# Expert value sums of a two-block network: which operand stands still in TensorE

## What is computed

```
def _peer(x, wq, k1, k2, u_tab, v_tab):      # x: 256 tokens x 1024; u_tab, v_tab: 16384 experts x 1024
    eidx, gate = ...                          # 8 heads x 16 chosen experts a token, softmax gates
    ub = jnp.take(u_tab, ib, axis=0)
    act = gelu(einsum('td,tkd->tk', xb, ub))
    vb = jnp.take(v_tab, ib, axis=0)
    return einsum('tk,tkd->td', gb * act, vb)
h = _layer_norm(ALPHA * h + _peer(h, ...), ln2_g, ln2_b)
```

## Time and profile before

| | us |
|---|---|
| median of three timed runs | 2996.52 |
| lowest, highest | 2991.83, 2996.59 |
| span of the profiled execution, first to last instruction | 2991.0 |
| TensorE matmuls busy | 2928.9 (98%) |
| TensorE weight loads busy | 2599.6 (87%) |
| VectorE busy | 2125.5 (71%) |
| ScalarE busy | 1498.7 (50%) |
| POOL busy | 686.6 (23%) |

### The profile page before, as it was taken

The page is one execution under the profiler, slowest core; times in us unless marked ns, Lnnn a source line. Parts: engine busy times, 40 slices in busy tenths (PEclk is TensorE's granted clock), DMA queues, the critical chain, the costliest instruction groups (busy, mean ns, idle before and its releaser), DMA issues.

```text
span 2991.0 us, 54746 instructions
## 1 busy us (share of the span) xinstructions
PE 2928.9 (98%) x18452; PEld 2599.6 (87%) x18452; DVE 2125.5 (71%) x3656; ACT 1498.7 (50%) x2410; POOL 686.6 (23%) x443
## 2 busy tenths in 40 slices
PE   8999999999999999999999999999999999999998
PEld 7888888888878888899999978888899999978887
DVE  6667576766766667758986677777758986767776
ACT  4456444444655445445555545455545555544544
POOL 0002100000021002117778400000207777500000
PEclk9999999999999999999999999999999999999999
DMA  6545455555463554457887777776446888777775
GB/s 222 189 162 187 159 167 186 169 189 189 148 219 119 184 185 149 155 174 206 197 212 186 194 253 241 242 239 195 165 160 198 195 208 199 179 245 243 239 243 189
DMA packets 255982, 581.52 MB, mean 194 GB/s; under 512 B 61336, under 2 KB 127168, under 8 KB 255344
## 3 DMA queue, kind: packets, MB, share of 16 engines
q1 hardware_dynamic: 210656, 547.94, 56.6%
q0 software_dynamic: 45200, 31.93, 7.0%
HBM read 542.92 MB, written 36.84 MB: 194 GB/s over the span
## 4 chain that ended last, share of the span: by engine, by line
PE 81%; DVE 12%; ACT 3%; issue 2%; DMA 1%; POOL 1%; SPq 0%; ACTq 0%; DVEq 0%
PE acc L783 32%; PE work L719 23%; PE work L729 10%; PE work L731 5%; DVE wsp L456 4%; PE acc L847 3%; PE acc L1203 2%; ACT wsp L453 2%; PE acc L1340 1%; DMA ring<-in_stream 1%; DVE rows_sb L2474 1%; ACT scratch L1419 1%; DMA back<-second_dram 1%; PE work L1125 0%; POOL st L583 0%
## 5 line engine op out<-in xcount | busy, mean ns | idle before, releaser
L456 DVE TENSOR_TENSOR wsp<-ring,wsp 128x1024 fp32r<-128x1024 f32 x908 | 1105.3, 1225 | 562.2 <-ACT wsp L453 558.0
L453 ACT ACTIVATE wsp<-ring 128x1024 fp32r<-128x1024 f32 x944 | 984.9, 1052 | 498.6 <-PE work L719 238.3
L719 PE MATMUL work<-xsp,wsp 128*128 128x256 f32 x7872 | 971.7, 285 | 6.2 <-DVE wsp L456 3.2
L783 PE MATMUL acc<-wsp,hsp 128*128 128x512 f32 x4128 | 956.0, 390 | 9.9 <-DVE hsp L2674 8.0
L719 PEld LDWEIGHTS work<-xsp,wsp 128*128 128x128 f32 x7872 | 953.8, 192 | 11.3 <-DVE wsp L456 4.8
L783 PEld LDWEIGHTS acc<-wsp,hsp 128*128 128x128 f32 x4128 | 769.2, 188 | 173.7 <-issue 9.6
L729 PE MATMUL work<-xsp,wsp 128*128 128x512 f32 x1408 | 503.8, 400 | 6.7 <-DVE xsp L1859 5.5
L687 POOL DMA_INDIRECT second_dram<-rows_sb,spots x256 | 472.9, 1847 | 146.3 <-issue 88.7
L731 PE MATMUL work<-xsp,wsp 128*128 128x256 f32 x1408 | 395.7, 281 | 0.0
L583 POOL TENSOR_TENSOR st<-st,mhalf 128x1 f32<-128x1 f32 x24 | 20.6, 864 | 1561.7 <-DVE st L1879 805.1
L729 PEld LDWEIGHTS work<-xsp,wsp 128*128 128x128 f32 x1408 | 265.2, 188 | 75.0 <-DVE xsp L1859 6.6
(11 more groups left out here) (355 smaller groups left out, 2138.9 us busy)
## 6 DMA issues: line engine op xcount, KB each, us to landing
ring<-in_stream SPq DMA_DIRECT2D x944, 512.0 KB
back<-second_dram SPq DMA_DIRECT2D x256, 128.0 KB, 3.2
second_dram<-back POOLq DMA_DIRECT2D x32, 512.0 KB, 13.3
second_dram<-arena SPq DMA_DIRECT2D x184, 64.0 KB
rows_sb<-in_rows POOLq DMA_DIRECT2D x10, 512.0 KB, 6.8
second_dram<-acts SPq DMA_DIRECT2D x72, 64.0 KB
second_dram<-rows_sb,spots POOLq DMA_INDIRECT x256
h_saved_dram<-h POOLq DMA_DIRECT2D x2, 1024.0 KB, 5.0
```

Of the source, the lines that this page charges most:

```text
L453: self.eng.activation(dst[:, 0, :], src, ACT.Copy).then_inc(high_done, 1)
L456: self.eng.tensor_tensor(dst[:, 1, :], src, dst[:, 0, :].bitcast(F32), ALU.subtract)\
L719: mm = pe.matmul(out_, lhsT=w[:, a, 128 * c:128 * c + 128], rhs=xsp[:, b, c, :], start=(c == 0 and n == 0), stop=(c == DC - 1 and n == 2))
L783: mm = pe.matmul(ACC[2 * b + n][:, :], lhsT=act[:, pa, 128 * b:128 * b + 128], rhs=w[:, pw, 512 * n:512 * n + 512], start=(first and m == ...
```

## The change

The expert layers' value stage gets its own unit, in the wide form. For each of the eight 128-column pieces c of the width, the high piece of the value unit is stationary and the 512 columns of `hsp` (high and low parts of 256 tokens) move; then the low piece is stationary and the 256 high columns move. So there are 8 pairs, 16 matmuls and 16 weight loads a unit, and the result lies with the width on the partitions: eight sums of 128 x 512, one in each of the eight banks. The stage therefore claims the four `W` banks too, before its first unit.

At the end three steps are new. ScalarE copies columns 256 to 511 of each bank, the part of the low activations, to `arena` (`second_half`). VectorE adds them to columns 0 to 255 (`columns_sum`). TensorE turns the eight sums back with 16 transposes of 128 x 128 into the four `ACC` banks, where `add_block` finds them as before. The last wait of `add_block` is now given by its caller. The other callers pass the same wait as before.

```diff
+        class ValueSum(Group):
+            def bank(self, c):
+                return ACC[(0, 2, 1, 3)[c]] if c < 4 else W[(self.k + c) % 4]
+            def claim_all(self, pe):
+                for q in range(4):
+                    self.claim(pe, q)
...
                 pe.wait_ge(g_moved, GROUPS * (l + 1))
+                G.claim_all(pe)
 
                 def value_unit(i, first, last, it=None):
                     n = 0 if it is None else it
                     pe.wait_ge(act_low, n * 6 + (TILES + NKEYS * l + i + 1))
-                    down_unit(G, i, hsp[:, i % 2, :, :], first, last, 6 * n)
+                    w = G.unit(pe, i, 6 * n)
+                    a = hsp[:, i % 2, :, :]
+                    for c in range(DC):
+                        o = G.bank(c)
+                        pe.matmul(o[:, :], lhsT=w[:, 0, 128 * c:128 * c + 128], rhs=a.rearrange("p s t -> p (s t)"),
+                                  start=first, stop=False)
+                        mm = pe.matmul(o[:, 0:T], lhsT=w[:, 1, 128 * c:128 * c + 128], rhs=a[:, 0, :],
+                                       start=False, stop=last)
+                        if last and c < DC - 1:
+                            mm.then_inc(ev("value_column"), 1)
+                    mm.then_inc(unit_done, 1)
...
+                for c in range(DC):
+                    G.wait_added(pe, max(c, 1), l)
+                    if c == 4:
+                        G.wait_added(pe, 3, l)
+                    n, k = c // 4, c % 4
+                    for b in range(NB):
+                        mm = pe.transpose(ACC[2 * b + n][:, 128 * k:128 * k + 128],
+                                          columns_sum[:, c, 128 * b:128 * b + 128], ident)
+                        if c == 3:
+                            mm.then_inc(ev("half_block"), 1)
+                        elif c == DC - 1:
+                            mm.then_inc(ev("value_turned") if b else ev("first_block"), 1)
...
                 split.upto(G.u + 129)
+                G = ValueSum(part, "V")
+                for c in range(DC):
+                    if c < DC - 1:
+                        act.wait_ge(ev("value_column"), (DC - 1) * l + c + 1)
+                    else:
+                        G.ready_unit(act, NKEYS - 1)
+                    act.activation(second_half[:, c, :], G.bank(c)[:, T:2 * T], ACT.Copy).then_inc(ev("half_copied"), 1)
                 ln_squares()
...
                 dve.wait_ge(h_back, 16 * (l + 1))
+                V = ValueSum(part, "V")
+                for c in range(DC):
+                    dve.wait_ge(ev("half_copied"), DC * l + c + 1)
+                    V.added(tt(columns_sum[:, c, :], second_half[:, c, :], V.bank(c)[:, 0:T], ALU.add), c)
                 dve.memset(st[:, 31:32], 0.0).then_inc(side_free, 1)
-                layer_norm(3 * l + 3, part, (V, NKEYS - 1))
+                layer_norm(3 * l + 3, part, lambda eng: eng.wait_ge(ev("value_turned"), l + 1))
```

26 lines of the change are left out of this document (19 added, 7 removed).

## The result

The changed kernel took 3026.4 us, the median of 4 runs (3023.29 to 3032.19); in the same series the kernel before took 2995.89 us (2991.83 to 2996.59). The ratio is 1.0105, 95% interval 1.0093 to 1.0117: 1.05% slower. The forecast was 3026.8.

A forecast was written before the change was run, and what follows sets the result against it. TensorE's matmul issue was taken to bound the value stage. Units 25.0, start 0, clock -1.6 and ends 6.9 add 30.3 us to the 2991.0 span; with 5.5 around it, 3026.8 us, range 3013 to 3037.

The forecast's parts named there:

- The units: Value units: eight long-short pairs at 0.3525 us make 2.82 us a unit against 2.72, adding 25.0 us in both layers.
- Rival (a): Value units: the mixed stream runs in its quicker rhythm, 0.347 us a pair, giving 3017 us; chance 20%.
- (b): Value units: bank changes and waits at a unit's head add time, giving 3039 us, or 3033 at half; chance 12%.
- (c): Value units: extra matmuls cost nothing, 0.340 us a pair, giving 3001.8 us; 6% stated for this and (d).
- (d): Value stage: the change misses its aim, for example because transfers bound it, giving 3002 us; 6% stated with (c).
- The start: Value stage's start: claiming the work banks delays the first units 1.7 us, hidden by a later transfer wait; cost 0.
- The clock: Second layer, after the stop ahead of unit 3: a stop about 1.5 us shorter keeps the clock up, -1.6 us.
- The ends: Value stages' ends: copies, sums and transposes delay the residual sums, 3.75 us in the first layer, 3.15 in the second.
- the lower of the two bounds: ScalarE's copies at the stage's end: one every 0.27 us, the quick limit of 0.27 to 0.42.
- the bound of 6.2: Value stages' ends: lowest added time, in us for both layers, if ScalarE's copies keep step in both.
- Around the span: Whole execution: 5.5 us between profiled span and median time, carried over unchanged.
- The sum: Whole kernel: all terms add 30.3 us to the span, giving 3026.8 us, 1.0% slower; chance 60% for its pair cost.

The follow-up runs named there:

- e6: Changed kernel with twelve 512-column table-stationary matmuls a value unit, leaving out some low pieces and adding low-part products: 2998.37 us, ratio 1.0007.
- e1: Changed kernel with each value unit's eight 512-column matmuls first and its eight 256-column ones after: 3023.25 us, ratio 1.0092.
- e4: Kernel before with four of a value unit's twelve matmuls cut in two, so eight long and eight short alternate: 3021.22 us, ratio 1.0078.
- e10: Changed kernel with two long and two short matmuls in turn instead of one and one: 3017.59 us, ratio 1.0076.
- e7: Kernel before with all twelve matmuls of a value unit cut in two, 24 of 256 columns: 3036.16 us, ratio 1.0136.
- e2: Changed kernel with each work bank claimed at its first use instead of all four ahead of the first value unit: 3022.6 us, ratio 1.0083.
- e12: Kernel before, unchanged, run and profiled a second time: 2996.52 us, ratio 0.9997.
- e11: Changed kernel, unchanged, run and profiled again with more timed runs: 3025.27 us, ratio 1.0105.
- e3: Changed kernel without the copies, sums and 16 transposes at each value stage's end, so the low-activation sum is left out: 3019.25 us, ratio 1.0075.
- e5: Kernel before with the transfers of gate blocks 4 and 5 requested some 6 us earlier: 2984.87 us, ratio 0.996.
- e9: Kernel before with gate blocks 4 and 5 requested early and POOL's reload of residual and norm rows held until gate block 16: 2986.91 us, ratio 0.9972.

## Why the prediction was right, point by point

**The units: the mechanism was right and the size was near.** I took 0.3525 us a pair from two feed-forward units, 25.0 us in both layers. The slow rhythm is 0.3533, 13.3 us a layer; the quick one is 0.3467, 6.7 us. A stage is in one of them, so the term was a mixture that I treated as one number. Each of the two profiles of the changed kernel has one stage of either kind, 20 us; both stages slow would be 26.7. Rival (a) was therefore not wrong either: it held in 2 of that kernel's 4 profiled stages. My reason for passing it over, that the quicker stretch of the earlier trace rows only follows a hitch, failed: whole stages of 960 pairs run at it without a stop. What each matmul costs is shown by three counts of matmuls over the same 6144 columns: 12 take 2.72 us (e6), 16 take 2.77 to 2.83 (the changed kernel, e1, e4, e10) and 24 take 2.88 (e7). 16 x 13.3 ns on 2.56 us is 2.773, the quick rhythm; the slow one adds 3.3 ns a matmul. Every one of these matmuls has a weight load of its own, so the runs do not tell a price of the matmul from a price of the load.

The Trainium skill (page "TensorE: Matmul & The Clock Gate", section "Back-to-back issue gap") has about 2.5 ns beyond the columns for a warm matmul taken by itself, and says that in a stream of long ones this is too much. The runs do not bear either out for this stream of a weight load with each matmul: 13.3 ns at 512 and at 256 columns. By the page's figure e7 would have cost 7.5 us; it cost 38.6.

**The rivals (b), (c), (d) fell.** Nothing waits at a unit's head (b). The extra matmuls are not free (c); e4, which does nothing but add them, was 25.4 us slower. The transfers do not bound the stage (d): the DMA share went down from 0.73 to 0.70 as the units grew longer.

**The start: 0 was forecast, 3.3 measured.** e2 takes the claim away, and unit 3 comes no earlier in sum than the scatter allows. Over the five profiles that keep the transfers' order and have no early claim (before, e12, e2, e4, e7) the distance from the stage before to unit 3 is 11.9 to 14.9 us, on the mean 13.4 in the first layer and 12.4 in the second; over the six with the claim (after, e11, e1, e3, e6, e10) it is 11.9 to 15.7, on the mean 14.3 and 13.1. By these means the claim would cost some 0.8 us a layer, about half of the 3.3, and the six and five values are too few to show even that; the other half is scatter, which is 3 us a layer. I missed that the claim's wait would be 1.9 to 2.9 us, not 1.7: ScalarE was itself waiting for a transfer into the ring.

**The clock: wrong.** I expected that a shorter stop would keep the clock up, -1.6 us. The stop ahead of unit 3 did shrink, by 1.6 and 1.7 us where I had about 1.5. But in the second layer, where it went from 4.28 to 2.58, the clock was at 0.50 behind it as before; it also fell behind the claim's stop in the first layer. The rows of stops are these (busy time by stretch, PE alone): the changed kernel behind the claim, first layer; e3 behind the claim, second layer, a stop of 1.85; the kernel before in e12 behind 3.92 and behind 3.33 us; e5 behind 2.29; e6 behind the claim, second layer, again 1.85.

```profile
1721.00:1724.00 3.00, 3.00 (x11) 0.50 0.64 191
```

```profile
2642.50:2645.50 3.00, 3.00 (x11) 0.50 0.81 252
```

```profile
2642.50:2645.50 3.00, 3.00 (x15) 1.00 0.65 193
1727.00:1730.00 3.00, 3.00 (x8) 0.50 0.49 166
```

```profile
1734.00:1737.00 3.00, 3.00 (x15) 1.00 0.91 276
```

```profile
2633.00:2636.00 3.00, 3.00 (x15) 1.00 0.84 277
```

It fell behind 1.85 and held behind 3.33 us, and behind 1.85 it did both. So the length of the stop alone, on which my step rested, does not decide. What does was not found.

The price is 1.6 us in the second layer before, but 2.8 us in e12's first layer (343.07 us from unit 3 to E against 340.27 in its second), where the clock was low twice as long. Over the eleven profiles named above, what a layer takes from unit 3 to E beyond 125 of its own units is 2.1 us on the mean without the early claim (0.1 to 2.9) and 0.6 with it (0.1 to 1.7). So a shorter stop ahead of unit 3 does seem to save clock time, about what the start costs: both together are 15.0 us a layer without the claim and 14.3 with it. The first profile of the kernel before, against which I summed, happened to pay the clock in one layer only.

**The ends: right.** +6.9 was forecast (3.75 and 3.15), 6.3 measured (3.3 and 3.0), and e3 removes 5.0 of it. Of the ScalarE copies the fifth starts 1.05 us behind the first, one every 0.26, at the lower of the two bounds where I had taken 0.33; the sums follow each other by 1.33 / 4 = 0.33, where I had 0.35. That is why it came out at the low end, near the bound of 6.2. The first layer's end came out 0.45 under its term, the second's 0.16; there the residual sums began at E + 0.80, a little ahead of the 1 to 2 us that I had named.

**Around the span.** I carried 5.5 us over, as time outside the span. It was 2.0; the other 3.5 were that the profiled execution was quicker than its kernel's median. For the forecast the two are the same, as long as the changed kernel's median is meant.

**The sum.** The forecast median, 3026.8, met 3026.4. Part of that is cancellation: in the profiled executions units and clock together gave 19.9 us against 23.4 in the sum, because one layer was quick; the ends gave 0.6 less; start and lead-in gave 5.7 more, for which I had set nothing. That the median came within 0.4 us is luck; the range is what the working supports.

## What to carry to other kernels

Where TensorE is full, count its matmuls as well as its columns: with one weight load each, every further matmul cost about 13 ns here at 512 and at 256 columns, and at 512 columns whichever operand was stationary. Before the arithmetic of a stage is rewritten, look at the order of transfers at its start; two requests moved some 6 us forward in each layer were worth 7 us in the traces and 12.7 in the medians, while the rewriting cost 30. If long and short matmuls must be mixed, two and two in turn may be worth trying: it took 7.7 us off the median here, of which the units explain 3.3. And compare profiled executions by their granted clock too: on the mean, the slower runs of one unchanged kernel were the ones with the lower clock.

## What the runs showed of the hardware that was not expected

A strictly alternating stream of 512- and 256-column matmuls runs at 346.7 or at 353.3 ns a pair, as a mean, and keeps to one of them over 960 pairs; the same program shows both, in either layer. Uniform streams have one rhythm (226.67 and 120.0 ns), and groups of two or of eight showed one each (348.5 and 349.3 a pair), in two stages each. What decides between the two was not found.

The granted clock fell to 0.50 behind stops of 1.85, 1.97 (e9), 2.58, 3.92 and 4.28 us and held behind stops of 1.85 (e6), 2.29, 3.11 and 3.33 us: in this range the length of a stop alone does not tell whether the clock falls.

How long a transfer takes near a stage's start hangs on what was requested just ahead of it. In the kernel before, gate blocks 2 and 3 landed 2.0 to 2.1 us behind their requests in both layers; blocks 4 to 6, requested 2 us later and right behind POOL's reload of the norm's rows, took 7.0 to 9.3 us, with the DMA share at 1.01 from 1718 to 1726. With the requests moved ahead (e5), or the reload put later (e9), TensorE's stop moved to another unit each time, and only the first of the two moves made the sum smaller.
